# GLA chunk loop of a two-block network: exponents ahead of the masked copies, diagonal scores and turned keys ahead of the output products, two key-row buffers

## The reference

```
bc = jnp.cumsum(gc, axis=1)
o_inter = jnp.einsum('bthd,bhde->bthe', qc * jnp.exp(bc), S)
decay = jnp.exp(jnp.where(causal, bc[:, :, None] - bc[:, None, :], -jnp.inf))
att = jnp.einsum('bthd,bshd,btshd->bhts', qc, kc, decay)
o_intra = jnp.einsum('bhts,bshe->bthe', att, vc)
S_new = exp(b_last) * S + einsum('bshd,bshe->bhde', kc * exp(b_last - bc), vc)
```

## Time and profile before

| | us |
|---|---|
| median of 3 runs | 2412.48 |
| their lowest and highest | 2412.28 and 2418.6 |
| the profiled execution's own time | 2416.19 |
| its span, first to last instruction | 2414.5 |
| PE matmul busy | 2278.6 (94%) |
| DVE / ACT / POOL busy | 1077.5 / 667.7 / 867.6 |
| granted PE clock, mean over the span | 0.966 |

### The profile page before, as it was taken

The page is one execution under the profiler, slowest core; times in us unless marked ns, Lnnn a source line. Parts: engine busy times, 40 slices in busy tenths (PEclk is TensorE's granted clock), DMA queues, the critical chain, the costliest instruction groups (busy, mean ns, idle before and its releaser), DMA issues.

```text
span 2414.5 us, 29324 instructions
## 1 busy us (share of the span) xinstructions
PE 2278.6 (94%) x12340; PEld 1959.7 (81%) x12340; DVE 1077.5 (45%) x1309; ACT 667.7 (28%) x1035; POOL 867.6 (36%) x501
## 2 busy tenths in 40 slices
PE   7999989899999999989999979899999999999898
PEld 7999967899998888868887658777877777777676
DVE  2899988500067766630026555222122222222643
ACT  3454351112245642210136634100000000000243
POOL 2789731332245535023275440333223223222100
PEclk9999989999978889999999989999999999999899
DMA  3111114211100023211220022121111111111211
GB/s 126 53 36 53 54 52 131 74 53 32 39 1 1 1 70 131 88 53 35 106 75 2 1 88 96 44 70 53 35 52 51 35 52 43 44 52 61 105 64 50
DMA packets 89610, 136.61 MB, mean 57 GB/s; under 512 B 6464, under 2 KB 71616, under 8 KB 89374
## 3 DMA queue, kind: packets, MB, share of 16 engines
q1 hardware_dynamic: 89502, 135.08, 16.6%
HBM read 118.26 MB, written 16.81 MB: 56 GB/s over the span
## 4 chain that ended last, share of the span: by engine, by line
PE 76%; POOL 8%; DVE 7%; ACT 4%; issue 4%; DMA 2%; SPq 0%; DVEq 0%; POOLq 0%; ACTq 0%
PE PS L359 61%; PE PS L2004 3%; PE PS L1047 2%; PE PS L1081 2%; PE PS L399 2%; POOL side_sum L539 2%; PE PS L2313 1%; PE PS L388 1%; PE PS L1675 1%; POOL pool_tmp L1899 1%; PE PS L1662 1%; PE PS L1688 1%; POOL arg_b L1270 1%; POOL arg_b L1269 1%; POOL mo_raw L1924 1%
## 5 line engine op out<-in xcount | busy, mean ns | idle before, releaser
L359 PE MATMUL PS<-xh,wh 128*128 128x512 f32 (+2 forms) x1664 | 523.3, 364 | 11.1 <-DVE xl L454 4.0
L359 PE MATMUL PS<-xl,wh 128*128 128x512 f32 (+2 forms) x1664 | 519.0, 362 | 0.0
L359 PE MATMUL PS<-xh,wl 128*128 128x512 f32 (+2 forms) x1664 | 517.0, 361 | 0.0
L342 POOL CAST wh<-raw 128x2048 fp32r<-128x2048 f32 x46 | 87.3, 1897 | 821.7 <-PE PS L359 737.5
L359 PEld LDWEIGHTS PS<-xh,wh 128*128 128x128 f32 x1664 | 312.0, 189 | 50.5 <-issue 5.8
L359 PEld LDWEIGHTS PS<-xl,wh 128*128 128x128 f32 x1664 | 311.8, 189 | 40.9
L359 PEld LDWEIGHTS PS<-xh,wl 128*128 128x128 f32 x1664 | 311.2, 189 | 39.7
L337 POOL TENSOR_TENSOR wl<-raw,wh 128x2048 fp32r<-128x2048 f32 x62 | 287.5, 4637 | 53.1 <-ACT wh L333 49.4
L359 PE MATMUL PS<-wh,xh 128*128 128x256 f32 (+1 forms) x784 | 229.5, 317 | 2.7 <-DVE wl L350 0.9
L359 PE MATMUL PS<-wl,xh 128*128 128x256 f32 (+1 forms) x784 | 228.4, 316 | 0.0
L359 PE MATMUL PS<-wh,xl 128*128 128x256 f32 (+1 forms) x784 | 227.9, 316 | 0.0
(11 more groups left out here) (331 smaller groups left out, 3460.6 us busy)
## 6 DMA issues: line engine op xcount, KB each, us to landing
h_rows<-rows SPq DMA_DIRECT2D x24, 512.0 KB, 2.6
rows<-h_rows SPq DMA_DIRECT2D x24, 512.0 KB, 3.3
raw<-in_w_ffn_down_dram SPq DMA_DIRECT2D x11, 1024.0 KB, 4.8
raw<-in_gla_w_in_dram SPq DMA_DIRECT2D x10, 1024.0 KB, 5.1
raw<-in_w_ffn_gate_dram SPq DMA_DIRECT2D x10, 1024.0 KB, 5.0
raw<-in_w_ffn_up_dram SPq DMA_DIRECT2D x10, 1024.0 KB, 5.0
raw<-in_conv_w_in_dram SPq DMA_DIRECT2D x16, 512.0 KB, 4.7
raw<-in_w_in_dram SPq DMA_DIRECT2D x8, 1024.0 KB, 5.5
```

The lines of the kernel that those rows point to most:

```text
L342: nc.gpsimd.tensor_copy(wh[slot][:], buf[:]).then_inc(unit_hi, 1)
L359: last = nc.tensor.matmul(out_of(c, cn), s, x[:, c0:c0 + cn], start=n == 0 and m == 0, stop=n == len(terms) - 1 and m == 2)
```

## The change

Four things are moved, and a buffer is added. No product, copy, activation or DMA of the result is left out; only the shapes of the squares' sources and one small extra activation are new.

1. DVE: `exponents(c + 1, 0)` stands ahead of both `weights(c, 0)` and `weights(c, 1)`, instead of between them.
2. ACT: exp of `arg_b` of the next chunk (`factors(c + 1, 1)`) stands at the end of the chunk, behind the copy of the outputs, and ahead of `q_decayed`. The exp table is fetched earlier by an exp of one column behind silu (L1164 of the changed kernel). Only two of the four squares are taken from PSUM ahead of the copy, the other two later from `v_rows`.
3. PE: the next chunk's diagonal scores and turned keys stand ahead of the output products. Ten r matmuls instead of six stand ahead of the pair products, and 24 instead of 28 behind them.
4. `k_rows` has two buffers, and ACT's copy to it stands ahead of the output squares.

On DVE, between the scans of chunk c + 1 and the state update. The first piece is the kernel before, `arg_a` and `arg_b` are the exponents of chunk c + 1, `att` the scores of chunk c.

```diff
--- before.py
+++ after.py
@@ -144,7 +144,7 @@
         decay = at("decay", [P, GH, P], Z0 + 41472)
         v_rows = at("v_rows", [P, NX, D], O0)
         k_decayed = at("k_decayed", [P, GH, P], S0 + 2 * SLOT)
-        k_rows = at("k_rows", [P, GH, P], S0 + 2 * SLOT + 2048)
+        k_rows = [at("k_rows0", [P, GH, P], S0 + 2 * SLOT + 2048), at("k_rows1", [P, GH, P], W0 + 6144)]
         att = at("att", [P, GH, P], S0 + 2 * SLOT + 4096)
         state = at("state", [P, GH, GV], S0 + 2 * SLOT + 6144)
         v_meta = at("v_meta", [META, D], S0 + 2 * SLOT + 6144)
@@ -1029,7 +1029,7 @@
             last.then_inc(kt_done, 1)
 
         R_STEPS = 3 * KT
-        R_FIRST, R_BETWEEN = 6, 2
+        R_FIRST, R_BEFORE, R_BETWEEN = 6, 4, 2
 
         def r_out(c, h):
 
@@ -1051,24 +1051,23 @@
         def gla_tensor(pe):
             pe.wait_ge(gv_left, 3 + 4 * NV_TILES)
 
+            def diagonal(c):
+                cols = slice(TILES[c][0], TILES[c][0] + P)
+                after(pe, diag_used, c - 1)
+                for h in range(GH):
+                    last = nc.tensor.matmul(PS[:, 3, h * P:(h + 1) * P], qk[:, GH + h, cols], qk[:, h, cols], start=True, stop=True)
+                last.then_inc(diag_done, 1)
+
             for c, (c0, n) in enumerate(TILES):
-                if 0 < c < NX:
-                    turn_keys(pe, c)
-                if c > 0:
-                    after(pe, diag_used, c - 1)
-                    for h in range(GH):
-                        last = nc.tensor.matmul(PS[:, 3, h * P:(h + 1) * P], qk[:, GH + h, c0:c0 + n], qk[:, h, c0:c0 + n],
-                                                start=True, stop=True)
-                    last.then_inc(diag_done, 1)
                 if c > 0:
                     if c == 1:
                         pe.wait_ge(unit_ready, U_GR + 1)
                     after(pe, r_left, 2 * (c - 2))
                     r_products(pe, c, 0, R_FIRST)
-                if 0 < c < NX:
-                    gate_logits(pe, c + 1)
-                if c > 0:
-                    at = R_FIRST
+                    if c < NX:
+                        gate_logits(pe, c + 1)
+                    at = R_FIRST + R_BEFORE
+                    r_products(pe, c, R_FIRST, at)
                     for g, group in enumerate(GROUPS):
                         if g == 0:
                             after(pe, o_kept, c - 1)
@@ -1084,7 +1083,11 @@
                             r_products(pe, c, at, at + R_BETWEEN)
                             at += R_BETWEEN
                     r_products(pe, c, at, 2 * R_STEPS)
-
+                if c < NX:
+                    diagonal(c + 1)
+                if c + 1 < NX:
+                    turn_keys(pe, c + 1)
+                if c > 0:
                     pe.wait_ge(qdec_ready, c)
                     pe.wait_ge(att_ready, 2 * c)
                     for h in range(GH):
@@ -1096,14 +1099,14 @@
                     after(pe, state_ready, c)
                     v = v_meta if c == 0 else v_rows[:, c - 1, :]
                     for h in range(GH):
-                        last = nc.tensor.matmul(out_bank(6, h), k_rows[0:n, h, :], v[:, h * GV:(h + 1) * GV], start=True, stop=True)
+                        last = nc.tensor.matmul(out_bank(6, h), k_rows[c % 2][0:n, h, :], v[:, h * GV:(h + 1) * GV], start=True, stop=True)
                     last.then_inc(s_done, 1)
 
         def copy_keys(act, c):
             n = TILES[c][1]
             act.wait_ge(kt_done, c + 1)
-            after(act, s_done, c)
-            nc.scalar.copy(k_rows[0:n].rearrange("p h t -> p (h t)"), PS[0:n, 0, :]).then_inc(k_rows_done, 1)
+            after(act, s_done, c - 1)
+            nc.scalar.copy(k_rows[c % 2][0:n].rearrange("p h t -> p (h t)"), PS[0:n, 0, :]).then_inc(k_rows_done, 1)
 
         def soft_parts(act, c):
 
@@ -1132,32 +1135,47 @@
             act.wait_ge(arg_ready, 2 * (c - 1) + g + 1)
             nc.scalar.activation(ARGS[g][:], ARGS[g][:], ACT.Exp, scale=1 / TAU).then_inc(arg_exp, 1)
 
+        def out_squares(act, c, heads):
+
+            for h in heads:
+                col = 4 * (c - 1) + h
+                x = out_bank(1, h) if h < 2 else v_rows[:, c - 1, h * GV:(h + 1) * GV]
+                act_own.step(act, nc.scalar.activation(o_junk[:], x, ACT.Square, accum_out=SS_O[:, col:col + 1]))
+
         def gla_scalar(act):
             for c, (c0, n) in enumerate(TILES):
-                if 0 < c < NX:
-                    copy_keys(act, c)
                 if c > 0:
                     nc.scalar.activation(q_decayed[:], decay[:], ACT.Exp, scale=1 / TAU).then_inc(qdec_exp, 1)
-                    factors(act, c, 1)
                 if 0 < c < NX:
                     soft_parts(act, c + 1)
                     act.wait_ge(bl_ready, c + 2)
                     if c + 1 < NX:
                         decays(act, c + 1)
+                if c > 1:
+                    act.wait_ge(o_kept, c - 1)
+                    out_squares(act, c - 1, range(2, GH))
+                if 0 < c < NX:
                     factors(act, c + 1, 0)
                 if c > 0:
                     act.wait_ge(r_tile, 2 * c)
                     for h in range(2):
                         after(act, r_used, 2 * (c - 1) + h - 1)
                         nc.scalar.activation(r_silu[h][:], r_out(c, h), ACT.Silu).then_inc(r_left, 1)
+                    nc.scalar.activation(stat[:, 94:95], stat[:, 93:94], ACT.Exp)
+                if c == 0:
+                    act.wait_ge(unit_ready, U_GR + 2)
+                if c + 1 < NX:
+                    copy_keys(act, c + 1)
                 if c > 0:
                     act.wait_ge(o_done, c)
-                    for h in range(GH):
-                        col = 4 * (c - 1) + h
-                        act_own.step(act, nc.scalar.activation(o_junk[:], out_bank(1, h), ACT.Square, accum_out=SS_O[:, col:col + 1]))
+                    out_squares(act, c, range(2))
                     if c < NX:
                         act.wait_ge(s_done, c + 1)
                     nc.scalar.copy(v_rows[:, c - 1, :], banks(1, 2)).then_inc(o_kept, 1)
+                if c < NX:
+                    factors(act, c + 1, 1)
+            act.wait_ge(o_kept, NX)
+            out_squares(act, NX, range(2, GH))
 
         def gate_early(dve, c):
 
@@ -1226,15 +1244,17 @@
                     gate_early(dve, c - 1)
                 if c < NX:
                     sums(c + 1)
-                for g in range(2):
-                    if c > 0:
-                        weights(c, g)
-                    if c == 0 and g == 1:
-                        dve.wait_ge(unit_ready, U_GR + 1)
-                        dve.wait_ge(gv_tile, GH * NV_TILES)
-                        split_unit_fast(dve, U_GR + 1, 1)
-                    if c < NX:
-                        exponents(c + 1, g)
+                if c < NX:
+                    exponents(c + 1, 0)
+                if c > 0:
+                    weights(c, 0)
+                    weights(c, 1)
+                else:
+                    dve.wait_ge(unit_ready, U_GR + 1)
+                    dve.wait_ge(gv_tile, GH * NV_TILES)
+                    split_unit_fast(dve, U_GR + 1, 1)
+                if c < NX:
+                    exponents(c + 1, 1)
                 if c < NX:
                     dve.wait_ge(s_done, c + 1)
                     dve.wait_ge(ebl_ready, c + 1)
```

## The result

| | before | changed |
|---|---|---|
| median of the runs | 2413.85 us (4 runs) | 2382.07 us (4 runs, 2380.06 to 2383.36) |
| profiled execution, its span | 2414.5 us | 2378.3 us |
| granted clock over the span | 0.966 | 0.982 |

The kernel before has four runs here, one more than before the prediction. The changed kernel is faster: the ratio of the runs is 0.9864, with a 95% interval of 0.9847 to 0.9881, or 33 us; the medians lie 31.8 us apart. The forecast was 2391.4 us, 21 us less than before; the time lies inside its range. Run again on another chip, the changed kernel took 2382.62 us, a ratio of 0.9882 (0.9863 to 0.9901).

What follows compares the result with a forecast made beforehand. It took PE's wait for `arg_b` and the low clock behind it as the losses, with the ACT and DVE chain taking over. Gains 2.7 + 15.0 + 3.4 = 21.1 us from 2412.5 gave 2391.4 us, range 2379 to 2406.

Steps and rivals of the forecast that it cites:

- Softplus parts at +4.65, `arg_b` at +4.2, pair products at +9.2: ACT and POOL, in us after a chunk's first output square: softplus parts start 2.1 us earlier than before.
- A gap of about 0.4 us leaves the clock up: PE ahead of the `arg_b` pair products: the wait of 2.26 us shrinks to about 0.4, assumed to leave the clock up.
- A new wait ahead of the outputs: PE ahead of the output products: it waits 2.4 us for `att`, complete at +19.3 us after the first square.
- the exchange on DVE leaves the sum up to the last masked copy as it is: DVE: all three groups precede the last masked copy in either order; `arg_a` comes 1.89 us earlier, but nothing waits for it.
- 1.1 us a chunk for a clock that falls at the outputs in half of the chunks: PE at the output products: half of a possible 2.1 us a chunk, making a chunk 24.0 us.
- PE's floor of about 19 us a chunk: PE without waits at full clock: 26.51 us, less 2.26 idle and 5.1 for the low stretch.
- First chunk 2.7 us, last 3.4: Gains at the loop's ends: first, between none and some 5 us; last, 2.1 + 1.9 minus 0.6 for a possible clock fall.
- all warm: Forecast's own lower end, the clock never falling: 22.9 us a chunk, gains 21.7 + 5 + 4, 2381.8 us.
- Rival A: PE's clock falls at every output product: 25.0 us a chunk, six gain 9.1, 2397.3 us in all; chance 17%.
- Rival B: DVE's `arg_b` exponents, slowed by POOL, hold up the next chunk and the old PE wait stays: 2404.5 us; chance 13%.
- C: Slower: PE's clock falls at the new wait and stays low through logits and pair products, +2.8 us a chunk, 2429 us; 7%.
- D: `att` binds at 26 us a chunk, so the shorter gap never shrinks PE's time: about 2411 us; chance 3%.

Runs made afterwards that it cites:

- Experiment 4: Changed kernel without the early exp of one column behind silu, so the exp table is fetched between output copy and exp of `arg_b`: 2408.77 us, ratio 0.9984.
- experiment 2: Changed kernel with POOL's product for `q_decayed` put ahead of its products for `arg_b`, so only `arg_b` comes late: 2418.03 us, ratio 1.0020 to the kernel before.
- experiment 3: experiment 2's kernel with 20 instead of 4 r matmuls between the logits and the pair products: 2387.07 us, ratio 0.9893 to the kernel before.
- Experiment 1: Changed kernel with DVE's order put back, masked copies of levels 0 to 3 ahead of the exponents of `arg_a`: 2390.76 us, ratio 0.9908.
- experiment 8: Changed kernel with PE's diagonal scores and turned keys back at the chunk's beginning, ACT's keys copy behind the output copy: 2394.11 us, ratio 0.9922.
- experiment 5: Kernel before with one exchange on ACT, exp of `arg_b` ahead of exp of `q_decayed`: 2410.39 us, ratio 0.9990.
- experiment 6: Kernel before with 22 instead of 6 r matmuls ahead of the logits and pair products, 12 instead of 28 at the end: 2419.57 us, ratio 1.0022.
- experiment 7: Changed kernel with only the next chunk's diagonal scores put back behind the increment products, turned keys staying ahead of the outputs: 2384.48 us, ratio 0.9890.
- experiment 11: experiment 10's kernel with the output copy ahead of `arg_b` in chunk 7, and 14 instead of 4 r matmuls in chunks 1 and 8: 2369.73 us, ratio 0.9821.
- experiment 9: Changed kernel with exp of `q_decayed` moved into ACT's wait ahead of the output copy: 2382.01 us, ratio 0.9875 to the kernel before.
- experiment 10: experiment 9's kernel with exp of `arg_b` too ahead of the output copy: 2380.23 us, ratio 0.9868 to the kernel before.

## Why the prediction was right, and where it was short

The direction and the mechanism held: the wait ahead of the `arg_b` products shrank, the clock stayed up behind it, and the chain through ACT and DVE took over. The gain was 33 us instead of 21, a little beyond the 31 us above which the prediction saw it with 3%. Step by step:

- *Softplus parts at +4.65, `arg_b` at +4.2, pair products at +9.2.* Right: +4.6, +4.2, +9.4. Experiment 4 shows that a single table load less on this way is worth 26 us.
- *A gap of about 0.4 us leaves the clock up.* Right for the clock, though the gap was 0.70 us: no low stretch in six chunks. Experiments 2 and 3 show it by making the gap long and short again. It was taken, not derived, and it had little to spare: in chunk 1 a gap of 1.15 us was followed by a fall.
- *A new wait ahead of the outputs.* Right in place, 0.87 us instead of 2.4. Here the sum failed in one term: "the exchange on DVE leaves the sum up to the last masked copy as it is", with 3.76 us for the eight exponents. They take 2.7, as they no longer meet POOL's `k_decayed` product; exponents and masked copies together take 763.70 - 757.08 = 6.62 us instead of 7.67. Experiment 1 undid the exchange, and the chain became 1.1 us a chunk longer and the time 8 us. The scans' part was 0.3 us shorter as well. So `att` was complete at +17.9, and 17.9 + 0.1 + 3.73 is the measured 21.74 us where the sum said 22.9.
- *1.1 us a chunk for a clock that falls at the outputs in half of the chunks.* It never fell: 0 measured. As a bound it was sound: with waits of 1.9 and 2.04 us (experiments 1 and 8) it does fall, in some chunks or most, for about 1.7 us each.
- *PE's floor of about 19 us a chunk.* Too low: the sum took half of the 10.2 us at the lower clock away. PE busy fell by 24.9 us in six chunks that had 57.8 us of low clock before, 0.43 of it, and at full clock PE is busy for 120.57/6 = 20.1 us a chunk. The floor did not bind, so nothing followed from this.
- *First chunk 2.7 us, last 3.4.* Measured (676.08 to the first square at 702.29, against 672.50 to 702.19) 3.5 and (16.65 - 14.32) 2.3. In the last chunk the wait for `arg_b` of 1.62 us still took the clock down, where the sum had it up for all three levels. The two errors cancel, and the first is luck besides. The kernel of experiment 5, whose order on PE is that of the kernel before, kept its full clock at the beginning of chunk 1 and took 699.71 - 674.37 = 25.3 us there, less than the changed kernel's 26.2; neither did the clock fall at that place in experiments 6 and 8, which have the same order on PE:

```profile
674.37:686.17 11.80, 9.98 (x75) 9.03 (x75) 8.93 (x13) 5.62 (x7) 4.89 (x7) 1.00 0.01 1
```

So no run shows that the change takes away the low stretch of chunk 1; its 3.5 us belong to the profiled execution of the kernel before, which at 2416.19 us was above the median.

The sum of the loop is 3.5 + 28.6 + 2.3 = 34.4 us. The prediction's 15.0 us for the six middle chunks was the mis-sized term: two errors of 1.1 us a chunk each, both on the same side. That the median lies next to the prediction's "all warm" bound of 2381.8 us is a coincidence: the bound had 21.7 us for the middle chunks and 9 us for the ends, where 28.6 and 5.8 us were measured.

Rival A (the clock falls at every output) did not come about: four transposes and a wait of 0.87 us, or of 1.73 in experiment 7, left the clock at 1.00. The Trainium skill ("TensorE: Matmul & The Clock Gate", Part 4: PE-mode transpose) says that transposes do not count as PE being busy in the same way. No run here has transposes long enough to test the rule itself, but next to a wait they were not what brought the fall: experiment 7 has them there and stayed up behind 2.17 us, experiment 8 has them elsewhere and fell in five of six chunks behind 2.04 to 2.10 us. Rival B's contention exists, but `arg_b`'s exponents ended in time. C and D did not occur.

Three things stay open. Why the clock falls after 1.9 us in some chunks and not in others of the same kernel was not separated; the length of the wait alone does not decide it (the first two points of the last section). No run here took ACT's split of the squares, or the second key-row buffer, alone, so their shares are not known. And the parts do not add up: taking back the early table, the order on PE or the order on DVE costs 26, 12 and 8 us, 46 together for a change worth 33, since each of them by itself can bring a wait back at which the clock falls.

## What to carry to other kernels

When an engine's clock depends on its activity, look for the wait ahead of each low stretch, not for idle time: here 2.3 us of waiting cost 4 to 5 us more behind it. Such a wait can be closed from either side, by earlier data or by independent work moved into it (experiments 3 and 11), but only down to the next chain, or it reappears there (experiment 6). And the order of two steps on one engine is not free when another engine's work beside them slows the one and not the other.

## What the runs showed of the hardware

- PE's waits and the clock behind them, ahead of the pair products. In chunks 2 to 7: 0.57 to 0.84 us, never a fall; 1.77, 1.88, 2.26 and 2.44 us, a fall in every one. In the first and the last chunk there are lengths between: 1.12 to 1.35 us in chunk 1 were followed by a fall in all nine profiles that have them; in chunk 8, 0.97 and 0.98 us (experiments 7 and 8) by none, 1.49 to 1.62 us by a fall (experiments 3 and 6, the changed kernel), but 1.70 us (experiment 9) by none.
- The same ahead of the outputs, between r matmuls and output products of 256 columns each, where the pair products have 64: 0.87, 1.07 and 1.73 us never; 1.90 us in three of five chunks, 2.04 us in five of six; 2.17 us once, without a fall (experiment 7); 4.63 us in every one.
- A low stretch behind a wait of 1.9 to 2.1 us ahead of the output products is 3.4 us long, one around the wait of 4.63 us 6.8 us; among pair products it is 6.8 to 10.2 us long, 13.7 us in the last chunk of experiment 10, and 20.3 us once.
- DVE's subtraction of two SBUF operands is held up by POOL's running product (1.52 against 0.42 us); the masked copy from PSUM is not (3.91 against 3.83 for seven). Four scans take 3.04, 3.27 or 3.65 us, the longer the more of POOL's products lie beside them (experiment 10, the changed kernel, experiment 9).
